# Two-layer encoder trunk: the third group of the dilated attention spread over every fourth step, and memory banks copied before token operands

## What is computed

```python
for i in range(2):                       # layer 0: mixer A, layer 1: mixer B
    q, k, v, mq, gate = split(x @ w_in[i])
    o_mix = mixer(q, k, v)               # 12 heads of width 128
    mk, mv = split(mem @ w_mkv[i])       # 256 memory tokens, 4 heads
    o_mem = softmax(mq @ mk.T / sqrt(128)) @ mv
    y = concat([o_mix, o_mem]) * silu(gate)
    x = layer_norm(ALPHA * x + y @ w_out[i])

def mixer_b(q, k, v):                    # three query groups share k and v
    for g, (window, dil) in enumerate([(128, 1), (512, 4), (2048, 16)]):
        outs[g], lse[g] = band_attention(dilate(rope(q[g]), dil), dilate(rope(k), dil),
                                         dilate(v, dil), window // (2 * dil))
    return einsum(softmax(lse over the groups), outs)
```

## Time and profile before

| | |
|---|---|
| median of 3 runs | 2128.75 us |
| the profiled execution | 2131.39 us, span 2129.6 us |
| mean granted TensorE clock | 0.998 |
| PE busy | 2092.9 us (98%) |
| DVE busy | 1599.4 us (75%) |
| ACT busy | 1076.5 us (51%) |
| memory stage | 0 to about 74.7 us |
| layer 0, pairs | about 74.7 to 650 us |
| layer 1, pairs | about 825 to 1950 us |

### The profile page before, as it was taken

How to read it: one execution, slowest core, us unless ns; L and a number is a source line. 1 busy time by engine, 2 the same in 40 slices (tenths; PEclk the granted TensorE clock), 3 DMA queues, 4 the chain that set the end, 5 groups by cost and what they waited for, 6 DMA issues and landing times.

```text
span 2129.6 us, 31595 instructions
## 1 busy us (share of the span) xinstructions
PE 2092.9 (98%) x10796; PEld 1752.7 (82%) x10796; DVE 1599.4 (75%) x3662; ACT 1076.5 (51%) x2646; POOL 18.4 (1%) x23
## 2 busy tenths in 40 slices
PE   7999999999999998999999999999999999999998
PEld 7888888888888886788888888888888888888887
DVE  5777877778665458868888888888888888777465
ACT  5544454545554234455555556555555565565321
POOL 0000000000000001000000000000000000000001
PEclk9999999999999999999999999999999999999999
DMA  8411111121126461213233133143243233315642
GB/s 250 122 49 37 50 60 50 58 62 40 55 85 226 149 204 55 71 54 96 67 93 87 57 102 97 55 110 86 65 110 82 69 101 81 105 52 182 223 158 94
DMA packets 242458, 204.99 MB, mean 96 GB/s; under 512 B 20852, under 2 KB 198076, under 8 KB 242300
## 3 DMA queue, kind: packets, MB, share of 16 engines
q1 hardware_dynamic: 242300, 202.97, 31.7%
HBM read 168.40 MB, written 34.52 MB: 95 GB/s over the span
## 4 chain that ended last, share of the span: by engine, by line
PE 80%; DVE 10%; DMA 4%; ACT 3%; issue 2%; SPq 1%; DVEq 0%; POOLq 0%; POOL 0%; ACTq 0%
PE bank L1177 15%; PE bank L1179 15%; PE bank L1178 15%; PE bank L1256 8%; PE bank L1228 7%; PE bank L1355 5%; PE bank L1353 5%; PE bank L1354 5%; DVE work L1683 4%; PE bank L1242 4%; DVE ring L1683 2%; DMA weight_scratch<-trig 1%; DMA work<-weight_scratch 1%; DVE work L1816 1%; ACT ring L1407 1%
## 5 line engine op out<-in xcount | busy, mean ns | idle before, releaser
L1177 PE MATMUL bank<-x_ops,ring 128*128 128x512 f32 (+1 forms) x1808 | 850.5, 470 | 12.0 <-issue 4.7
L1179 PE MATMUL bank<-x_ops,ring 128*128 128x512 f32 (+1 forms) x1808 | 698.9, 387 | 0.0
L1178 PE MATMUL bank<-x_ops,ring 128*128 128x512 f32 (+1 forms) x1808 | 696.6, 385 | 0.0
L1683 DVE SCALAR_TENSOR_TENSOR ring<-raw,ring 128x512 fp32r<-128x512 f32 x368 | 251.2, 685 | 213.9 <-ACT ring L1407 213.2
L1505 ACT COPY work<-bank 128x256 f32<-128x256 f32 (+2 forms) x448 | 164.6, 367 | 466.9 <-PE bank L1242 465.9
L1179 PEld LDWEIGHTS bank<-x_ops,ring 128*128 128x128 f32 x1808 | 340.8, 188 | 71.0
L1177 PEld LDWEIGHTS bank<-x_ops,ring 128*128 128x128 f32 x1808 | 345.4, 191 | 54.1 <-issue 9.8
L1178 PEld LDWEIGHTS bank<-x_ops,ring 128*128 128x128 f32 x1808 | 345.4, 191 | 33.0
L1407 ACT CAST ring<-raw 128x512 fp32r<-128x512 f32 x368 | 227.2, 619 | 164.9 <-PE bank L1355 146.1
L1256 PEld LDWEIGHTS bank<-work 128*128 128x128 f32 x1744 | 262.0, 190 | 48.6 <-ACT work L1505 5.9
L1522 ACT ACTIVATE work<-work,soft 128x256 f32<-128x256 f32 (+2 forms) x448 | 226.7, 506 | 97.3 <-DVE soft L1864 95.3
(11 more groups left out here) (86 smaller groups left out, 2173.3 us busy)
## 6 DMA issues: line engine op xcount, KB each, us to landing
raw<-in_w_in_b SPq DMA_DIRECT2D x160, 256.0 KB, 3.1
raw<-in_w_out SPq DMA_DIRECT2D x112, 256.0 KB, 3.4
raw<-in_w_in_a SPq DMA_DIRECT2D x80, 256.0 KB, 3.1
work<-weight_scratch SPq DMA_DIRECT2D x24, 768.0 KB, 5.2
y_scratch<-work SPq DMA_DIRECT2D x32, 512.0 KB, 2.9
x_ops<-y_scratch SPq DMA_DIRECT2D x64, 256.0 KB, 4.7
work<-v_scratch SPq DMA_DIRECT2D x48, 256.0 KB, 4.6
raw<-in_w_mkv SPq DMA_DIRECT2D x32, 256.0 KB, 4.9
```

Of the source, the lines that this page charges most:

```text
L1177: nc.tensor.matmul(dst, w_h, x_h, start=start, stop=False, skip_group_check=again)
L1178: nc.tensor.matmul(dst, w_h, x_l, start=False, stop=False, skip_group_check=again)
L1179: return nc.tensor.matmul(dst, w_l, x_h, start=False, stop=stop, skip_group_check=again)
L1683: return nc.vector.scalar_tensor_tensor(out=dst, in0=a, scalar=1.0, in1=b, op0=ALU.mult, op1=op)
```

## The change

Three things are changed, in order and place alone; no instruction is added or removed.

Group 2 of every head but the last starts at pair 3i + 3 step 23 with gap 4, where it started at pair 3i + 4 step 2 (T = 30) with gap 3. Its last tile stands at T = 51 both ways.

In the memory stage the four banks are ordered by half of the width first (bank i: token tile i % 2, half i // 2), PE waits for two banks ahead of stage 0 and for four ahead of stage 1, and the splits of piece 0 stand behind the second bank on ACT and DVE. ACT copies the finished banks (L1643, L1649, L1651) ahead of the token operands of that stage and no longer behind them.

In the first pair of layer 0 operand 4 and its third token sum are made at step 4 (DVE 4 and 5), operand 6 at step 8 (DVE 9).

```diff
-            job = add_job(1, 3 * i + 4, 2, tiles=b_tiles(2), order=tuple(range(TILES)),
+            job = add_job(1, *((3 * i + 3, 23) if i < HEADS - 1 else (3 * i + 4, 2)), tiles=b_tiles(2),
+                          order=tuple(range(TILES)),
                           values=chunks_of(b_vbuf[2]), rows=(rows_16_in, 32 * (i + 1)),
                           out=b_o[2], group=2, whole=False, stat=2,
-                          gap=3 if i < HEADS - 1 else 2,
+                          gap=4 if i < HEADS - 1 else 2,
...
             def memory_projection():
                 for i in range(4):
-                    pe.wait_ge(mem_in[i // 2], 16)
-                    rows_to_columns(mem_bank(i), mem_rows[:, i // 2, (i % 2) * HALF:(i % 2 + 1) * HALF])
-                pe.wait_ge(mem_lo, 4)
+                    pe.wait_ge(mem_in[i % 2], 16)
+                    rows_to_columns(mem_bank(i), mem_rows[:, i % 2, (i // 2) * HALF:(i // 2 + 1) * HALF])
                 for n in range(MKV_STAGES):
...
                     pe.wait_ge(w_lo, n + 1)
+                    if n < 2:
+                        pe.wait_ge(mem_lo, 2 * n + 2)
...
                     for i in range(4) if T in (4, 8) else ():
-                        x_high(0, 6 if T == 4 else 4, i)
+                        x_high(0, 4 if T == 4 else 6, i)
...
             def memory_projection():
                 for i in range(4):
                     memory_hi(i)
-                for n in range(AHEAD):
+                    if i == 1:
+                        split_hi(0)
+                for n in range(1, AHEAD):
                     split_hi(n)
                 for n in range(MKV_STAGES):
...
                     split_hi(n + AHEAD)
-                    for j, i in x_during(n):
-                        if j == 0:
-                            b11_in_full(0, i)
-                        x_high(0, j, i)
                     if n % 4 == 1:
...
                         nc.scalar.copy(mem_out[head % 2][:, MEM:2 * MEM], SB[head % 2][:, 0:MEM]
                                        ).then_inc(mv_free, 1)
+                    for j, i in x_during(n):
+                        if j == 0:
+                            b11_in_full(0, i)
+                        x_high(0, j, i)
...
-                    for i in range(4) if T == 8 else ():
+                    for i in range(4) if T == 4 else ():
                         third_token_sum(0, i)
                     for i in range(4) if T in (5, 9) else ():
-                        x_low(0, 6 if T == 5 else 4, i)
+                        x_low(0, 4 if T == 5 else 6, i)
...
                 for i in range(4):
                     memory_lo(i)
-                for n in range(AHEAD):
+                    if i == 1:
+                        split_lo(0)
+                for n in range(1, AHEAD):
                     split_lo(n)
```

More of the change, by code:

```diff
@@ L1410, in memory_hi @@
                 act.wait_ge(xt_ready, i + 1)
-                nc.scalar.copy(mem_cols[:, 0, 4 * (i % 2):4 * (i % 2) + 4, (i // 2) * P:(i // 2 + 1) * P],
+                nc.scalar.copy(mem_cols[:, 0, 4 * (i // 2):4 * (i // 2) + 4, (i % 2) * P:(i % 2 + 1) * P],
                                mem_bank(i)).then_inc(mem_hi, 1)
@@ L1726, in memory_lo @@
             def memory_lo(i):
-                part = slice(4 * (i % 2), 4 * (i % 2) + 4)
-                cols = slice((i // 2) * P, (i // 2 + 1) * P)
+                part = slice(4 * (i // 2), 4 * (i // 2) + 4)
+                cols = slice((i % 2) * P, (i % 2 + 1) * P)
                 dve.wait_ge(mem_hi, i + 1)
```

## The result

| | before | changed |
|---|---|---|
| median | 2128.14 us (8 runs) | 2134.56 us (7 runs, 2133.26 to 2135.21) |
| the profiled execution | 2131.39 us | 2133.26 us |
| ratio, 95% interval | | 1.003 (1.002 to 1.0041) |

The change makes the kernel 0.3% slower, 6.4 us. The forecast was 2126.2 us in a range of 2122.5 to 2130.0.

What follows compares the result with a forecast made beforehand. PE works without a break from 90 us, so the gain was expected in the memory stage and first pair: 2.0 + 0.5 + 0 = 2.5 us off 2128.75 gives 2126.2 us, range 2122.5 to 2130.0.

Steps and rivals of the forecast that it cites:

- Group 2, the waits: Layer 1, 11 heads: tiles 0 and 1 at group 1's end stay covered, nothing else moves; 0 us.
- Rival (a): Layer 1 near T = 30: PE waits each head for tile 0's copy, at most 8.8 us, 2135 us; chance 0.08.
- The cover of 0.1 to 0.2 us: Group 2, T = 30: tile 0's copy ends near 1025.8, PE uses it at 1025.9, so no wait.
- Group 2, PE: Layer 1: a tile costs PE 0.60 us whatever its gap; 0, with +-1.1 us over 11 heads.
- Stage 0: Memory stage: starts near 9.6, 1.7 us earlier, hidden by the full DMA queue; costed at nothing.
- Stage 10: Memory stage: keys' copy done at about 30.1, DVE's split ends last, start at 30.6, 1.6 us earlier.
- The copies: Memory stage, L1643: 1.04 us at the first wait plus 0.5 in each of two rounds; 2.0 us.
- rival (b): Memory stage: DVE limits the rounds, the 0.37 wait only moves; 1.04 + 0.5 gained, 2127.2 us; chance 0.14.
- Product 4: First pair of layer 0: operand 4's low parts made earlier; 0.8 to win less 0.3, 0.5 us (0.2 to 1.3).
- The start together: Memory stage and first pair: 2.0 + 0.5, 2.5 us less.
- Rival (c): Start: DMAs issued earlier land earlier, so 1.7 us comes on top of 2.5; 2124.6 us; chance 0.11.
- Rival (d): Layer 1: fewer tiles per stretch leave ACT and DVE less behind; 4 us less, 2122 us; chance 0.12.

Runs made afterwards that it cites:

- e2: Kernel before with group 2 alone moved (pair 3i + 3 step 23, gap 4); 2136.06 us, ratio 1.0039.
- e3: Changed kernel with ACT's cast ahead of the exponential for group 2's spread tiles only; 2122.22 us, ratio 0.9974.
- e11: Kernel before with ACT's cast ahead of the exponential for all jobs with a gap of three or more; 2123.19 us, ratio 0.9978.
- e9: Kernel before with only the banks' new order and ACT's copies L1643, L1649, L1651 ahead of the token operands; 2126.23 us, ratio 0.9994.
- e1: Changed kernel with group 2 as before (pair 3i + 4 step 2, gap 3); 2125.38 us, ratio 0.999.
- e5: Changed kernel with group 2's statistics one step later (T = 56 instead of T = 55); 2135.1 us, ratio 1.0033.
- e6: e1 with stage 0 behind all four banks again, the banks' new order kept; 2124.92 us, ratio 0.9989.
- e8: Kernel before with only the banks' new order and the early stage 0; 2127.03 us, ratio 0.9996.
- e4: Changed kernel with group 2 started one step earlier (step 22 instead of 23, gap 4); 2124.59 us, ratio 0.9986.
- e7: e3 with stage 0 behind all four banks again; 2122.11 us, ratio 0.9972.
- e10: e7 with ACT's cast ahead of the exponential for all jobs with a gap of three or more, both layers; 2122.35 us, ratio 0.9974.
- e12: e10 with group 2 put back where it was before the change; 2120.2 us, ratio 0.9962.

## Why the prediction was wrong

**The step that failed** is in "Group 2, the waits", its last sentence: "Nothing else moves: statistics, their DMAs and SP's waits keep their steps". The steps did stay. But I had worked out the waits of the tiles at the start, where DVE and ACT are loaded by group 1's end, and had taken it that a last tile at the same step T = 51 is ready at the same time. Tile 7 also keeps its step, T = 51, and its exponential its own, T = 53; what changed is what the queues of ACT and DVE had behind them when they came to it. The term was put at 0, and it measured 8.5 us (e2): the casts wait behind exponentials that wait for DVE's masks, DVE waits for the casts, and PE pays at T = 55 and T = 75.

It could have been read before the run: exponentials at T = 23 + 4k + 2 and casts at T % 4 == 1 are the same steps, 8 of 8 instead of 2 of 8. ACT's calls run in the order written, so on a shared step the cast waits for what the exponential waits for. The earlier trace rows gave the exponential its 0.40 us; what I left out is the idle time ahead of it, 1.08 us in the rows of after.

**Rival (a)** had the sign and nearly the time (2135 against 2134.6), but not the place, so the nearness of its time is luck. It put the wait at the copy of tile 0 near T = 30; no such wait came (L1257 on L1507 has 0.6 us in three places, all at T = 20, before 1.2 in six), and T = 30 takes 0.84 us in after and in e3 alike. The cover of 0.1 to 0.2 us held. Its chance, 0.08, was given for that place alone; that a slower case could come from any of the eight tiles was not counted.

**Group 2, PE**, 0 with 1.1 to either side: right. With the casts first in both, PE's rows from T = 23 to the end of T = 55 take 28.34 us a head where the group is moved (e3) and 28.27 where it is not (e11), 0.8 us over 11 heads: 0.21 more a head up to T = 54, and 0.14 less at T = 55.

**Stage 0**: right in time (9.6, measured 9.84) and in being hidden, but not in the cover. I had written that an earlier issue only stands in the queue, at no cost. It had a cost, the clock behind the longer wait: over 1 us at stage 10, of which perhaps 0.4 is left at the first pair.

**Stage 10**: 30.6 forecast, 32.03 in after. With the low clock stage 9 began at 30.16 (28.32 before), and stage 10 behind it. Where stage 0 was not early, stage 10 began at 30.43 to 31.35, which is about what the chain of the prediction gave.

**The copies**: 2.0 forecast, 2.16 in e9, the rounds 0.5 shorter as taken: 8.93 (44.12 to 53.05) before, 8.38 (42.56 to 50.94) in e9. So rival (b) fell. By the Trainium skill's page Perfetto Trace Analysis, section Identifying the Most-Contended Engine, the engine of highest occupancy is to be optimised first; I had read that as a limit that only less work on DVE would move. Nothing was taken off DVE, and the trace disagrees with that reading. The row of 0.37 us idle was the better guide.

**Product 4**: 0.5 forecast, 0.25 measured, of which the giving back was named, with 0.3 (0.37 measured).

**The start together**: 2.5 us forecast; layer 1 begins 1.92 earlier in after, and e1's median is 2.2 under its before. Part of the nearness is luck: the early stage 0 took something from the 2.16 of the copies, and product 4 brought half of what was forecast.

**Rival (c)** did not happen, since stage 9 began later than before and not earlier. Rival (d) had fewer tiles per stretch relieve ACT and DVE. Its time, 2122, is that of e3, but not for its reason: PE's waits in heads 1 to 11 go down from the 2.0 us of the earlier trace rows with the casts first, to 0.4 us both where group 2 is moved (e3) and where it isn't (e11).

## What to carry to other kernels

When a periodic job is moved, lay its steps against every other periodic job in the same queue, and do it for all its items, the last before all. Where two meet, put first the one that waits for nothing: here it was worth about 12 us to the changed kernel (e3) and 4.8 to the one before (e11). A wait that PE shows is where a delay surfaces, not where it is made; moving the place that shows it (e5) left the time as it was.

## What the runs showed of the hardware

Behind a wait of PE of 2.54 us the granted clock was 0.51 over 3 us (after, 25 to 28 us), and with no such wait 1.00 (e6). Behind the shortest such wait, 2.11 us in e8, it was 0.58. It isn't the wait's length alone that decides what it costs. Near the start of layer 1 all 14 traces have a wait of 1.73 us and some 6 us later a second one. Before, the second was 3.00 us, ended at 840.84, and the low clock came behind it, with work to slow; in e3 a wait of 3.02 us ended at 838.70 and the clock stayed at 1.00. Before, then e3:

```profile
840.00:842.00 2.00, 1.16 (x3) 1.00 (x4) 1.25 (x3) 1.96 (x4) 0.00 (x0) 0.68 0.00 0
842.00:844.00 2.00, 2.00 (x7) 1.52 (x6) 2.00 (x5) 1.08 (x2) 0.00 (x0) 0.50 0.22 60
```

```profile
838.00:840.00 2.00, 1.30 (x6) 1.11 (x7) 1.25 (x3) 1.91 (x5) 0.00 (x0) 1.00 0.00 0
840.00:842.00 2.00, 2.00 (x11) 1.63 (x9) 2.00 (x5) 1.81 (x4) 0.00 (x0) 1.00 0.31 85
```

Head 0 of layer 1 takes 86.12 us in the first and 85.26 in the second. The 14 traces fall into three kinds. In six (after, e1, e5, e8, e9, e11) the low clock came behind the wait of 1.73 us; the slowed work ran into the second wait, which was only 1.42 or 1.43 us long, and the head took 85.01 to 85.08. In six (before, e2, e4, e6, e7, e10) it came behind the second wait, of 3.0 us, and the head took 86.05 to 87.11. In two (e3, e12) it came behind neither: 85.26 and 85.02. e1 and e6 have the same order there and differ by 1.6 us. So a low clock ahead of a wait cost nothing here, and between two kernels one or two microseconds of this sort can come or go with nothing changed there; what decides it these runs don't tell.
